# Index scores first, two of three searches moved beside the attentions, and a weight ring that lends four places

## The reference

```python
z = rmsnorm(x, mix_norm) @ w_in
(aq, ak, av, iq, ik, iw, bq, bk, bv, bg, br, cu, dcq, dckv, dkpe) = jnp.split(z, ...)
# a: for each query the 128 best keys by an index score, then attention over these
s = relu(einsum('bthd,bsd->bths', iqb, ik) * idx_scale)      # 8 index heads
score = where(causal, einsum('bths,bth->bts', s, wb), -inf)
_, sel = top_k(score, 128)                                    # a mask in the kernel
y_a = attention(q, k, v over sel, with a relative bias)       # 4 heads of 64
y_b = gated linear attention(bq, bk, bv, bg, br)              # 4 heads, chunks
h = a * sigmoid(gate)                                         # cu = (a, gate)
y_c = silu(rmsnorm(depthwise_conv31(h) + b_dw, g_norm))
y_d = causal attention(queries from cq, keys and values from ckv, rope)
x = x + concat(y_a, y_b, y_c, y_d) @ w_out
```

## Time and profile before

| | us |
|---|---|
| median of 3 runs | 4423.96 (4423.77 to 4424.57) |
| the profiled execution | 4422.99 |
| its span, first to last instruction | 4421.7 |
| first mixer, phase 1, 2437.1 to 2645.8 | 208.7 |
| first mixer, phase 2, 2645.8 to 2803.9 | 158.1 |

### The profile page before, as it was taken

One profiled execution on the slowest core, in us unless ns is written; L12 is line 12 of the kernel. 1 busy time (PEld: TensorE's weight loads), 2 busy tenths in 40 slices (PEclk: granted clock), 3 DMA queues, 4 the chain that ended last, 5 costly groups with the idle time before them and its releaser, 6 DMA issues.

```text
span 4421.7 us, 47194 instructions
## 1 busy us (share of the span) xinstructions
PE 4083.1 (92%) x19301; PEld 3228.3 (73%) x19301; DVE 2271.7 (51%) x3546; ACT 1364.9 (31%) x2134; POOL 153.0 (3%) x294
## 2 busy tenths in 40 slices
PE   7659999999999999999999967999999997789999
PEld 6648887666678888887877754788788775557877
DVE  5745998777724444443332784433233238644332
ACT  3243322333333333332221323322232223233221
POOL 8000000000000000000000001000000000010000
PEclk9679999999999999999999977999999998789999
DMA  3002454555556666662332210133323321102332
GB/s 110 1 10 86 111 146 133 164 183 184 181 188 195 191 191 191 192 192 80 96 100 76 75 44 23 45 97 97 96 81 95 100 77 53 59 1 72 96 100 72
DMA packets 253337, 473.56 MB, mean 107 GB/s; under 512 B 15857, under 2 KB 138897, under 8 KB 250945
## 3 DMA queue, kind: packets, MB, share of 16 engines
q1 hardware_dynamic: 253120, 470.53, 35.0%
HBM read 399.96 MB, written 70.52 MB: 106 GB/s over the span
## 4 chain that ended last, share of the span: by engine, by line
PE 79%; DVE 13%; ACT 3%; POOL 2%; issue 1%; DMA 1%; SPq 0%; DVEq 0%; ACTq 0%; POOLq 0%
PE ps L352 23%; PE ps L354 23%; PE ps L353 23%; POOL arena L1138 2%; DVE arena L1824 2%; PE ps L455 1%; DVE arena L2729 1%; DVE wtwo L343 1%; DVE st L2727 1%; DVE arena L1138 1%; PE ps L2220 1%; DVE arena L2639 1%; DVE arena L1820 1%; DVE arena L1821 1%; PE ps L2248 1%
## 5 line engine op out<-in xcount | busy, mean ns | idle before, releaser
L343 DVE TENSOR_TENSOR wtwo<-wraw,wtwo 128x1024 fp32r<-128x1024 f32 x414 | 506.8, 1228 | 803.5 <-ACT wtwo L333 803.5
L352 PE MATMUL ps<-XH,wtwo 128*128 128x512 f32 (+1 forms) x1936 | 784.1, 405 | 1.3 <-DVE XL L481 1.3
L354 PE MATMUL ps<-XH,wtwo 128*128 128x512 f32 (+1 forms) x1936 | 755.3, 390 | 0.0
L353 PE MATMUL ps<-XL,wtwo 128*128 128x512 f32 (+1 forms) x1936 | 754.3, 390 | 0.0
L333 ACT ACTIVATE wtwo<-wraw 128x1024 fp32r<-128x1024 f32 x414 | 435.8, 1056 | 424.0 <-PE ps L354 412.7
L343 DVE TENSOR_TENSOR wlast<-wraw,wlast 128x1024 fp32r<-128x1024 f32 x204 | 249.9, 1228 | 397.9 <-ACT wlast L333 397.8
L354 PEld LDWEIGHTS ps<-XH,wtwo 128*128 128x128 f32 x1936 | 364.9, 188 | 77.2
L352 PEld LDWEIGHTS ps<-XH,wtwo 128*128 128x128 f32 x1936 | 366.0, 189 | 66.2 <-issue 2.2
L353 PEld LDWEIGHTS ps<-XL,wtwo 128*128 128x128 f32 x1936 | 366.7, 189 | 62.4
L352 PE MATMUL ps<-XH,wlast 128*128 128x512 f32 x912 | 378.8, 415 | 0.8 <-DVE wlast L343 0.8
L353 PE MATMUL ps<-XL,wlast 128*128 128x512 f32 x912 | 363.3, 398 | 0.0
(11 more groups left out here) (460 smaller groups left out, 6638.7 us busy)
## 6 DMA issues: line engine op xcount, KB each, us to landing
wraw<-in_ut SPq DMA_DIRECT2D x128, 512.0 KB, 4.2
wraw<-in_v SPq DMA_DIRECT2D x128, 512.0 KB, 4.0
wraw<-in_ffn_gate SPq DMA_DIRECT2D x88, 512.0 KB, 3.5
wraw<-in_ffn_up SPq DMA_DIRECT2D x88, 512.0 KB, 3.5
wraw<-in_ffn_down SPq DMA_DIRECT2D x88, 512.0 KB, 3.5
acts<-arena SPq DMA_DIRECT2D x128, 256.0 KB, 4.5
gates<-arena SPq DMA_DIRECT2D x16, 2048.0 KB, 9.1
arena<-gates SPq DMA_DIRECT2D x32, 1024.0 KB, 8.2
```

Of the source, the lines that this page charges most:

```text
L343: ve.e.tensor_tensor(W.items[n][8], W.rawof(n), W.items[n][7], ALU.subtract).then_inc(*ve.up("wlo", n))
L352: mm(out, lh, rh, start=start, stop=False)
L353: mm(out, lh, rl, start=False, stop=False)
L354: return mm(out, ll, rh, start=False, stop=stop)
```

## The change

In both mixers:

- The projections of the index (`iq`, `ik`) come before those of the convolution (`cu`), in the plan and on every engine. Scores go into three buffers (`SCO[1]` to `SCO[3]`), and all twelve score steps come before the first search. `order1` puts two of them behind each of the next projections; convolution, head norms and index then go on together ("pcxch") from the step `aqk` on.
- Phase 1 ends after 21 index steps: the scores and the first search. The other 18 steps stand in phase 2, one at the end of a round.
- The parts of "a" no longer wait for ("m", l). Each unit waits for ("m", l, i), its own block's mask, and `order2` holds back a unit until its mask stands ahead of it.
- The convolution's generators have 22 steps instead of 17: steps without work stand between its norm's hand-overs.
- Attention "a" keeps its exponentials and their transposes in lent memory, so the ring lends four places of six; two pieces of w_out may be split during phase 2. The border between the phases then splits one piece (place 1) where it split three.
- SP sends the gate weight, the rope tables and `uq` in phase 1, behind the loads of `br`.
- In "d" the eight matmuls of the queries come in rounds 1 and 2, those of keys and values in rounds 3 and 4, where each round had one block of both.
- The mask's running count is a scan of the equal flags with themselves (add, then maximum) instead of with a tile of ones.

```diff
 class Weights:
-    RAW, PAIRS, AHEAD = 3, 6, 4
+    RAW, PAIRS, AHEAD, LENT = 3, 6, 4, 4
...
             if n in self.lends:
-                split = max(split, n + self.AHEAD)
+                split = max(split, n + self.PAIRS - self.LENT)
...
                 pe.wait_ge(*at(*ready))
+                if self.mask:
+                    pe.wait_ge(*at(*self.mask, i))
...
     def order1(self):
-        steps = {"p": 18, "c": 17, "x": 3 * 13 + 1, "h": 2}
-        needs = {"c": 4, "x": 7, "h": 8}
+        steps = {"p": 18, "c": 22, "x": 3 * 4 + 3 * 9, "h": 2}
+        needs = {"c": 7, "x": 3, "h": 8}
...
-            for b in "pxxxcxxxh":
+            for b in "pxxh" if done["p"] < 7 else "pcxch":
...
     def pe_conv(self):
-        for _ in range(16):
+        for _ in range(17):
             yield
         pe.wait_ge(*at("csq", l))
...
-            ve.after().tensor_tensor_scan(WK[:, 0:nk], ONE[:, 0:nk], E, 0.0, ALU.mult, ALU.add).then_inc(*ve.up())
+            ve.after().tensor_tensor_scan(WK[:, 0:nk], E, E, 0.0, ALU.add, ALU.max).then_inc(*ve.up())
...
-            ve.after().tensor_tensor(MR[:, i, 0:nk], E, k.CM[:, 512 - nk:512], ALU.min).then_inc(*ve.up())
-            yield
-        ve.note("m", l)
+            ve.after().tensor_tensor(MR[:, i, 0:nk], E, k.CM[:, 512 - nk:512], ALU.min).then_inc(*ve.up("m", l, i))
+            yield
...
-            if done["x"] == steps["x"]:
+            if done["x"] >= 12 + 9 * min(max((done["a"] - 5) // 4 + 1, 0) // 2, 3):
                 step("a")
```

More of the change, by code:

```diff
@@ L2182, in plan_mixer @@
     plan_T(k, ("ik", l), w2, 1024)
+    for m in range(4):
+        plan_T(k, ("cu", l, m), w2, 1848 + 128 * m)
     plan_tok(k, ("aqk", l), w2, 0, 512)
@@ L2410, in order1 @@
                     done[b] += 1
-        self.left = steps["x"] - done["x"]
+        assert done["x"] >= 12
+        self.done_x = done["x"]
         return out
@@ L2430, in pe_proj1 @@
         yield
+        for m in range(4):
+            pe_proj(k, ("cu", l, m), XH, XL, 0, 5)
+            yield
         pe_tok(k, ("aqk", l), 512, XH, XL, AT4, 0, 5)
@@ L2499, in toks @@
             ac.note("tks", key)
-        for m in range(4):
-            even(m, ("cu", l, m), self.CU[:, m])
-            yield
         for m in range(2):
@@ L2515, in ac_proj1 @@
         yield
+        for m in range(4):
+            even(m, ("cu", l, m), self.CU[:, m])
+            yield
         toks(("aqk", l), 512, (self.AQ, 0, 256), (self.AK, 256, 512))
@@ L2555, in odd @@
                 ve.note("pj", key)
-        for m in range(4):
-            odd(m, ("cu", l, m), self.CU[:, m])
-            yield
         for m in range(2):
@@ L2564, in ve_proj1 @@
         yield
+        for m in range(4):
+            odd(m, ("cu", l, m), self.CU[:, m])
+            yield
         splits(k, split_ve, ("aqk", l), 512)
@@ L2599, in pe_conv @@
         last.then_inc(*pe.up("css", l))
+        for _ in range(3):
+            yield
         o = k.open(7, 8, "crow", l)
@@ L2672, in pe_index @@
                     yield
-            for _ in range(9):
-                yield
     def ac_index(self):
@@ L2723, in ve_index @@
                     yield
+        for i in range(1, 4):
+            nk = 128 * (i + 1)
+            s = self.SCO[i]
             ve.wait_ge(*at("causal", l, i))
@@ L2859, in pe_d, with queries @@
         k, pe, at, l = self.k, self.k.pe, self.k.at, self.l
-        for i in range(4):
+        def queries(i):
             s = slice(128 * i, 128 * i + 128)
@@ L2870, in pe_d @@
             pe.wait_ge(*at("latent", l, 2))
-            pe.e.matmul(o, self.CKV[:, 0, s], self.UKV, start=True, stop=True).then_inc(*pe.up("ukvd", l, i))
-            yield
+            pe.e.matmul(o, self.CKV[:, 0, 128 * i:128 * i + 128], self.UKV, start=True,
+                        stop=True).then_inc(*pe.up("ukvd", l, i))
+        queries(0)
+        queries(1)
+        yield
+        queries(2)
+        queries(3)
+        yield
+        keys(0)
+        keys(1)
+        yield
+        keys(2)
+        keys(3)
+        yield
         yield
@@ L3276, in sp @@
         k, l = self.k, self.l
-        for m in range(4):
-            load(k, ("cu", l, m))
         for m in range(2):
@@ L3281, in sp @@
         load(k, ("ik", l))
+        for m in range(4):
+            load(k, ("cu", l, m))
         splits(k, load, ("aqk", l), 512)
```

77 lines of the change are left out of this document (46 added, 31 removed).

## The result

The changed kernel takes 4436.45 us (median of nine runs, 4426.43 to 4438.83) against 4423.96 in the same session: a ratio of 1.0023, 95% interval 1.0012 to 1.0033. It is slower by 10 us (by the ratio) to 12 us (by the medians); the forecast was 6 us faster.

What follows compares the result with a forecast made beforehand. PE bounds the long stages, DVE phase 1 of the mixers, small steps and then PE phase 2. Per layer -28 + 25 = -3, two layers -6: 4422.99 - 6 = 4417, by the median 4418 us; range 4380 to 4446.

Steps and rivals of the forecast that it cites:

- the term for the ring: Around w_out: lending four of six places leaves two items split ahead instead of four; cost 0.
- rival 1: Phase 2, rounds 10 to 18: PE and DVE take turns, 51 us instead of 36.8; 4446 us, chance 0.19.
- Phase 1: First part of each mixer: 180.4 us against 208.7, giving back 28 us per layer, ends 16 and 44.
- the wait for the copies of the index key: Phase 1: PE still waits for these copies before the first scores, 3.2 us.
- the groups of scores: Phase 1: twelve pairs of scores in five groups between projections add 6.5 us, ends 3 and 14.
- the wait at the squares: Phase 1: PE stands at the convolution's squares for 9.4 us; with a low-clock restart 11, ends 0 and 20.
- Phase 2: Second part of each mixer, from 158.1 to near 183 us: growth 25 per layer, bounds 0 and 44.
- my allowance of 4.5 over DVE's sum: Phase 2, round 10 to the scores of block 2: 36.8 us, 4.5 above DVE's sum, for scores of two rounds.
- The query weight: Start of phase 2: sending uq in phase 1 removes about 10 us of DVE's waiting per layer.
- Rival 2: Mixers: the searches hide in waits between steps and the stall at csq doesn't come; 4380 to 4390 us, chance 0.27.
- Rival 4: Mixers: phase 1 stays DVE's and phase 2 takes what it is given; 4420 to 4428 us, chance 0.03.
- Rival 3: Phase 2, rounds 7 to 18: match_replace blocks POOL, +5 to +11 us per layer; 4428 to 4440 us, chance 0.04.

Runs made afterwards that it cites:

- e1: The kernel before with only the ring's split changed, so that it lends four places (wlast) and keeps two (wtwo); 4447.25 us, ratio 1.0061.
- b2: The changed kernel with the query weight uq sent where it was before, behind the loads of w_out; 4462.4 us, ratio 1.0091.
- m2: The changed kernel with 14 of 16 passes left out of the second and third search; 4398.1 us, ratio 0.9946.
- b3: The kernel before with wlast starting at a multiple of 128 and the mixers' unused 8-word tiles gone; 4388.1 us, ratio 0.9925.
- e6: The changed kernel with wlast starting at a multiple of 128 and the mixers' unused 8-word tiles gone; 4388.4 us, ratio 0.9914.
- e5: The kernel before with wlast 24 words longer, so that it starts at a multiple of 128; 4395.9 us, ratio 0.9940.
- b1: e6 with phase 1 reordered: convolution ahead of the projection, four first-search steps before the convolution ends, five behind; 4345.05 us, ratio 0.9822.
- e4: The kernel before with 32 bytes ahead of wtwo and 32 behind it, wtwo then at 45216; 4470.3 us, ratio 1.0107.
- e2: The kernel before with wlast 8 words longer, so that it starts at a multiple of 64; 4415.4 us, ratio 0.9982.

## Why the prediction was wrong, step by step

**The step that failed** is the term for the ring under "The rest": "`lend` now gives four of six places [...] Cost 0". It priced the splits that the lending moves and nothing else. The splits did cost nothing: from the first product with w_out to the next norm it is 47.9 us after and 48.2 before. But the lending also decides in which tensor the weights lie, and "the change leaves them alone", said of PEER and the feed-forwards, was false. By rows of the trace of before the term was to be had: 2928 more weights at 6.5 ns (19 us), 1008 more streamed tiles of PEER at 5 ns (5), 576 of the feed-forwards' down products at about 10 (6), together 30 (an estimate). The third line of `three` for the latter two, over the whole span:

```profile
L354 PE MATMUL ps<-wtwo,AL 128*128 128x512 f32 x688 | 268.1, 390 | 0.0
...
L354 PE MATMUL ps<-wtwo,HL 128*128 128x512 f32 x448 | 174.3, 389 | 0.0
...
L354 PE MATMUL ps<-wlast,HL 128*128 128x512 f32 x256 | 102.7, 401 | 0.0
```

e1 measures 24, the profiles 27 and more outside the mixers. With the term the forecast would have been 4418 + 30 = 4448; the measured 4436 lies between, since the mixers did better than forecast. None of my rivals had this mechanism; the measured sign matched rival 1 (slower), and its reason did not occur.

**Phase 1: right.** 180.4 forecast, 182.4 measured. Its terms: the wait for the copies of the index key 3.2, measured 3.07; the groups of scores 6.5, measured 2.8 us of waits (the last one below) and a part of what the clock of 0.96 takes from 77.87 busy; the wait at the squares 9.4, measured 10.84 and 10.65; DVE's work 111, measured 114.4 (30.82 + 62.53 + 21.04). PE's need at full clock, by the same working from the three windows of phase 1, is 156 where 153.2 stood.

```profile
2472.06 0.27 PE L2478 MATMUL ps<-ident,arena 8*128 8x8 f32 x1 [3.07 <-ACT arena L2518]
...
2509.11 1.61 PE L2694 MATMUL ps<-arena 32*128 32x512 f32 x4 [0.68 <-ACT arena L2708]
```

**Phase 2: the mechanism right, its growth forecast at twice what it was.** Forecast 25, measured 13 in the first mixer; the 171.2 us lie just under the 172 that the prediction named as a sign of being wrong. Rounds 1 to 9 up to the mask of block 2 took 68.7 where 72.5 stood, rounds 10 to the scores of block 2 33.2 for 36.8, the rest 69.3 for 73.9. The rows on DVE's queue: the mask of block 2, the scores of block 2 (DVE waited 3.06 for PE there before), the last mask.

```profile
2702.57 0.56 DVE L2767 TENSOR_TENSOR MR<-arena,CM 128x384 fp32r<-128x384 f32 x1
...
2736.26 0.96 DVE L2297 TENSOR_REDUCE st<-ps 128x2 f32<-128x768 f32 x1 [1.20 <-PE ps L2226]
...
2742.64 0.69 DVE L2767 TENSOR_TENSOR MR<-arena,CM 128x512 fp32r<-128x512 f32 x1
```

In rounds 10 to 18 the two queues overlapped: DVE 30.24 busy and PE 27.55 at 0.55 in 33.20. So rival 1 (they take turns, 51 us) is false, and my allowance of 4.5 over DVE's sum was too large (33.2 against a sum of 32.3). The same holds behind the third search: I added 5 us for a clock that recovers late, and it was at 1.00 there.

**The query weight: right.** 10 us per layer forecast; b2 gives 13 by the medians, and 7 to 10 if its profile's fall of the clock is taken off.

**Rival 2 (the searches hide): half true.** m2 shows 19 of 38 us not hidden; the forecast had 25.

**Rival 4 (the change doesn't do what it says): false.** Phase 1 fell by 26 us, and PE is busy for 142.7 of its first 148.6 us.

**Rival 3 (match_replace blocks POOL): false.** POOL's products of 48 and 80 columns, in the changed kernel beside passes of the third search (the first lies whole within a `match_replace`, which is the first row), then in the kernel before without them:

```profile
2722.82 0.68 DVE L2751 MATCH_REPLACE8 arena<-st,arena 128x512 f32<-128x512 f32 x1
...
2722.89 0.29 POOL L3139 TENSOR_TENSOR arena<-arena 128x48 f32<-128x48 f32 x1 [0.69 <-ACT arena L3092]
...
2725.76 0.35 POOL L3139 TENSOR_TENSOR arena<-arena 128x80 f32<-128x80 f32 x1 [0.84 <-ACT arena L3092]
```

```profile
2727.94 0.29 POOL L3091 TENSOR_TENSOR arena<-arena 128x48 f32<-128x48 f32 x1 [0.41 <-ACT arena L3044]
...
2730.59 0.36 POOL L3091 TENSOR_TENSOR arena<-arena 128x80 f32<-128x80 f32 x1 [0.84 <-ACT arena L3044]
```

They take the same. The rule of the Trainium skill ("SBUF — State Buffer", Who interferes with whom), that a VectorE instruction with at most one SBUF input outside the two-port modes does not contend with GpSimd, agrees with this if `match_replace` counts as one with a single input. Its row names two tiles, `st` and `arena`, so the row alone would not have told; the measured 0.29 us does.

**In sum:** the mixers were forecast at -6 us in all. They gave -11 by the medians and -17 by the profiles from e1 to the changed kernel, -23 by the profiles from the kernel before, and between -8 and 0 on equal ground (b3 to e6), where e6's two falls of the clock hide some 13. The ring, forecast at 0, took 24 to 36. The errors in the mixers, which were forecast too slow, were outweighed by one term that was left out.

## What to carry to other kernels

When a change alters where a tensor lies or how large it is, every instruction that reads it is part of the change: group the long stages' products by operand before calling them untouched, and look for two groups of one shape with different means. Give tiles that PE reads a start that 128 divides; a few padding words were worth more here (27 us in e5 and 35 in b3 on the kernel before, 48 in e6 on the changed one) than the rescheduling as it first stood; with its order mended (b1) that was worth 43. When one engine waits in a merged queue, look at what the same engine does just behind the wait: the work that made it late may fit there.

## What the runs showed of the hardware

- The record of a 128x512 product in fp32r lasted 389 ns in the feed-forwards with weights from a start that 128 divides (e5), and 395 to 397 from one that is 32 (e4), 64 (e2) or 96 (before) bytes past it; in the trace of before the starts of such products were 227 and 234 ns apart. With the streamed tile of PEER it was 389 ns at 0 (e5), 389 to 394 at 64 (e2) and 393 to 399 at 96 (before). Starts that are odd multiples of 128 were measured, multiples of 256 were not.
- The loss follows the start, not the region: `wlast` shed it by moving 96 bytes (-27 us on the whole kernel), and `wtwo` took it on by moving 32 (+47 us, with the arenas 64 bytes further on).
- The granted clock some 20 us ahead of the end of a phase of small products fell to 0.50 (1.2 GHz) in both mixers of e6 and b2 and in the first of b1, and stood at 1.00 (2.4 GHz) in b1's second and in the changed kernel, with the same work at that place. The fall made the phase 6.4 to 8.4 us longer; what decides it was not found.
- `max` and `match_replace` on DVE did not lengthen POOL's products (0.29 us for 48 columns beside them and without them).
